# Conditioning by halves of the features, and the first four projections by chunks of features in four banks at once

## The reference

```
mod_l = silu(c) @ w_ada + b_ada          # 6 x 1024 values: shift, scale, gate, twice
mod_c = silu(c_ctx) @ w_ada + b_ada      # the same for 256 context tokens
hl = rms_norm(x, g_mix_norm) * (1 + sc1) + sh1
pl = hl @ w_in                           # queries, keys, values, Fourier part
hc = rms_norm(ctx, g_mix_norm) * (1 + csc1) + csh1
pc_kv = hc @ w_in[:, keys and values]
```

## Time and profile before

| | |
|---|---|
| time, median of 3 runs | 2213.22 us (2210.96 to 2216.42) |
| the profiled execution | 2213.58 us, of which the span of instructions is 2211.9 us |
| TensorE busy | 2134.6 us (97%) |
| VectorE busy | 1215.4 us (55%) |
| ScalarE busy | 702.6 us (32%) |
| data moved | 434.71 MB, mean 197 GB/s |
| first matmul of a projection | 37.77 us after the start |

### The profile page before, as it was taken

The page is one execution under the profiler, slowest core; times in us unless marked ns, Lnnn a source line. Parts: engine busy times, 40 slices in busy tenths (PEclk is TensorE's granted clock), DMA queues, the critical chain, the costliest instruction groups (busy, mean ns, idle before and its releaser), DMA issues.

```text
span 2211.9 us, 24806 instructions
## 1 busy us (share of the span) xinstructions
PE 2134.6 (97%) x9914; PEld 1428.7 (65%) x9914; DVE 1215.4 (55%) x1726; ACT 702.6 (32%) x1059; POOL 148.8 (7%) x157
## 2 busy tenths in 40 slices
PE   7999998997999989999999999999999999999997
PEld 3454444333333335678888888878777788888886
DVE  1776863344433336895474555566986646343434
ACT  4123422110000005323242231346884424232331
POOL 0011100002310004000000000000110000000000
PEclk9999999999999999999999999999999999999999
DMA  9756465999999993211345454423342222222221
GB/s 389 288 185 215 142 241 208 401 427 427 420 426 426 428 427 127 79 68 62 133 160 186 156 177 163 143 77 116 126 156 81 96 95 77 95 95 95 95 96 57
DMA packets 112808, 434.71 MB, mean 197 GB/s; under 512 B 7982, under 2 KB 13106, under 8 KB 98760
## 3 DMA queue, kind: packets, MB, share of 16 engines
q1 hardware_dynamic: 92872, 361.46, 42.6%
q0 software_dynamic: 19840, 71.93, 9.0%
HBM read 430.57 MB, written 6.36 MB: 198 GB/s over the span
## 4 chain that ended last, share of the span: by engine, by line
PE 60%; PEld 15%; DVE 7%; DMA 7%; issue 6%; ACT 2%; DVEq 2%; POOLq 0%; SPq 0%; PEldq 0%; POOL 0%; ACTq 0%
PE PS L1132 7%; PE PS L740 6%; PE PS L743 6%; PE PS L744 6%; PE PS L840 6%; PEld PS L740 5%; PEld PS L744 5%; PEld PS L743 4%; DMA work<-in_w_dn 4%; PE PS L1155 4%; PE PS L1399 3%; PE PS L1403 3%; PE PS L1402 3%; PE PS L1169 2%; PE PS L969 2%
## 5 line engine op out<-in xcount | busy, mean ns | idle before, releaser
L744 PE MATMUL PS<-work_f32r,work_f32r 128*128 128x512 f32 x1168 | 454.4, 389 | 0.0
L2155 DVE TENSOR_TENSOR ring_f32r<-ring,work_f32r 128x2048 fp32r<-128x2048 f32 x100 | 227.8, 2287 | 140.5 <-ACT work_f32r L1553 140.1
L740 PE MATMUL PS<-work_f32r,work_f32r 128*128 128x512 f32 x768 | 299.5, 390 | 2.1 <-DVE work_f32r L2902 1.1
L743 PE MATMUL PS<-work_f32r,ring_f32r 128*128 128x512 f32 x768 | 298.8, 389 | 0.0
L1553 ACT ACTIVATE work_f32r<-ring 128x2048 fp32r<-128x2048 f32 x100 | 190.2, 1910 | 304.0 <-DMA ring<-in_mlp_w 247.0
L744 PEld LDWEIGHTS PS<-work_f32r,work_f32r 128*128 128x128 f32 x1168 | 219.3, 188 | 45.6
L1132 PE MATMUL PS<-work 128*64 128x512 f32 x752 | 170.6, 597 | 2.2 <-ACT work L1761 2.2
L740 PEld LDWEIGHTS PS<-work_f32r,work_f32r 128*128 128x128 f32 x768 | 144.2, 188 | 33.3 <-DVE work_f32r L2902 1.5
L743 PEld LDWEIGHTS PS<-work_f32r,ring_f32r 128*128 128x128 f32 x768 | 144.2, 188 | 29.8 <-issue 0.2
L740 PE MATMUL PS<-h_f32r,work_f32r 128*128 128x512 f32 x400 | 155.9, 390 | 1.4 <-DVE work_f32r L2175 1.4
L743 PE MATMUL PS<-h_f32r,ring_f32r 128*128 128x512 f32 x400 | 155.6, 389 | 0.0
(11 more groups left out here) (423 smaller groups left out, 3357.8 us busy)
## 6 DMA issues: line engine op xcount, KB each, us to landing
work<-in_w_gu SPq DMA_DIRECT2D x47, 2048.0 KB, 21.9
ring<-in_mlp_w SPq DMA_DIRECT2D x64, 1024.0 KB, 5.2
work<-in_w_dn SPq DMA_DIRECT2D x24, 2048.0 KB, 24.6
ring<-in_w_gu SPq DMA_DIRECT2D x16, 2048.0 KB, 24.2
work<-in_ada_w_2T POOLq DMA_DIRECT2D x48, 512.0 KB, 3.6
work<-in_ada_w_2T POOLq DMA_DIRECT2D x16, 1536.0 KB, 6.8
ring<-in_m_w_in SPq DMA_DIRECT2D x20, 1024.0 KB, 5.2
work<-in_w_adaT POOLq DMA_DIRECT2D x8, 2048.0 KB, 10.4
```

The costliest lines, as they stand in the source:

```text
L740: mm = nc.tensor.matmul(PS[:, bank + k, :], f32r(w_of), f32r(hi(c)), start=first and c == 0, stop=False)
L743: nc.tensor.matmul(PS[:, bank + k, :], f32r(wlo), f32r(hi(c)), start=False, stop=False)
L744: mm = nc.tensor.matmul(PS[:, bank + k, :], f32r(w_of), f32r(lo(c)), start=False, stop=last and c == 3)
L2155: tt(f32r(ring[:, s, at, :]), ring[:, s, at, :], f32r(tiles[s][:, at, :]), ALU.subtract).then_inc(w_split, 1)
```

## The change

The conditioning is done in two halves of the features: transfers q = 0, 1 bring shift and scale for chunks 0 to 3 (q = 0 the upper four chunks of rows of `w_ada`, q = 1 the lower), q = 2, 3 for chunks 4 to 7. The columns of `w_ada` are reordered on the host to that end, and a row piece is 4 KB where it was 8 KB. The halves of the first `w_in` tile are issued after q = 1 and after q = 3. Each group of four matmuls covers two chunks of rows, so shift and scale come out as two partial sums that VectorE adds. The first norm takes the form of the later ones, but with a bank and a semaphore count of its own. The first four projections run over chunks in the outer loop and over the four banks in the inner one; the conditioning of the second half lies among them on TensorE, after chunks 1, 2 and 3. The context norm's sum follows all four. POOL's first loads of `w_adaT` wait for the last of the conditioning matmuls, as before.

```diff
-        w_early = [wk(2048, 2, 4 * TN), wk(6144, 2, 4 * TN), wk(20224, 2, 4 * TN), wk(24320, 2, 4 * TN)]
+        w_early = [wk(at, 4, 2 * TN) for at in (2048, 6144, 20224, 24320)]
...
-            load_tile(0, 0, 0, columns(A["w_in"]))
+            for q in range(4):
+                load_early(q)
+                if q % 2:
+                    half = q // 2
+                    sp.dma_start(ring[:, 0, 4 * half:4 * half + 4, :], rows(A["w_in"])[:, 4 * half:4 * half + 4, 0:TN]) \
+                        .then_inc(tile_loaded[half], 16)
...
-            pool.wait_ge(mod_mm, 1)
+            pool.wait_ge(mod_mm, COND + 2)
...
+            def first_norm():
+                for c in (0, KC - 1):
+                    if c:
+                        pe.wait_ge(sq_ready, KC)
+                    else:
+                        pe.wait_ge(sq_added, 1)
+                    for q in range(TC):
+                        nc.tensor.matmul(PS[32 * q:32 * q + 32, 6, 0:P], ones[:, 0:32], h[:, c, q * P:(q + 1) * P], start=(c == 0),
+                                         stop=(c > 0))
+                pe.drain().then_inc(ms_done, 1)
+                pe.wait_ge(in_small, 16 * 5)
+                pe.wait_ge(rstd_ready, 1)
+                for q in range(TC):
+                    mm = nc.tensor.matmul(PS[:, 7, q * P:(q + 1) * P], eye[:, 32 * q:32 * q + 1].broadcast_to([P, P]), inv_q,
+                                          start=True, stop=True)
+                mm.then_inc(mod_mm, 1)
+
+            def condition(q):
+                cols_half, rows_half = divmod(q, 2)
+                pe.wait_ge(in_mod[q], 16)
+                if q == 2:
+                    pe.wait_ge(mod_evac_and_spread, 1)
+                for c in range(4 * rows_half, 4 * rows_half + 4):
+                    for shift_or_scale in range(2):
+                        group = 2 * (c % 2) + shift_or_scale
+                        nc.tensor.matmul(PS[32 * group:32 * group + 32, 4, :], c_cols[:, c, :],
+                                         w_early[q][:, c % 4, shift_or_scale * TN:(shift_or_scale + 1) * TN],
+                                         start=(c < 2), stop=(c >= KC - 2))
+                if rows_half:
+                    pe.drain().then_inc(mod_mm, 1)
+
+            def conditions_turned(cols_half):
+                pe.wait_ge(mod_evac_and_spread, cols_half + 1)
+                if cols_half:
+                    pe.wait_ge(mods_ready, 1)
+                for b in range(4):
+                    mm = nc.tensor.transpose(PS[:, 5, b * P:(b + 1) * P], mod_rows[:, b * P:(b + 1) * P], eye)
+                mm.then_inc(mod_mm, 1)
+
             pe.wait_ge(consts_set, 1)
-            norm_sum(0, h, T)
-
+            keep_warm(3, 8)
             pe.wait_ge(cond_ready, 1)
...
+            first_norm()
+            condition(0)
+            keep_warm(3, 9)
+            condition(1)
+            keep_warm(3, 5)
+            conditions_turned(0)
+            keep_warm(3, 6)
...
-            features(0, 0, 0, h, T, 0)
-            features(1, 0, 1, h, T)
+            for c in range(KC):
+                if c % 4 == 0:
+                    pe.wait_ge(tile_loaded[c // 4], 16)
+                pe.wait_ge(h_ready, c + 1)
+                for e in range(4):
+                    mm = nc.tensor.matmul(PS[:, e, :], ring[:, 0, c, e * P:(e + 1) * P], h[:, c, :], start=(c == 0), stop=(c == KC - 1))
+                    if c == KC - 1:
+                        mm.then_inc(qkv_mm, 1)
+                if c == 1:
+                    condition(2)
+                elif c == 2:
+                    condition(3)
+                elif c == 3:
+                    conditions_turned(1)
             norm_sum(1, csq, CTX)
-            features(2, 0, 2, h, T)
-            features(3, 0, 3, h, T)
             tile_done()
...
-            norm_root(0, T)
-            act.wait_ge(mod_mm, 1)
-            copy(mod_rows, PS[:, 4, :]).then_inc(mod_evac_and_spread, 1)
-            act.wait_ge(mods_ready, 1)
-            norm_affine(0, h, gain[:, 0, :], mod1[:, 0:KC])
+            root_table(0)
+            act.wait_ge(ms_done, 1)
+            nc.scalar.activation(std_q, PS[:, 6, 0:P], ACT.Sqrt, scale=1.0 / D, bias=eps6).then_inc(std_ready, 1)
+            for cols_half in range(2):
+                act.wait_ge(mod_mm, COND + 2 * cols_half)
+                copy(mod_rows, PS[:, 4, :]).then_inc(mod_evac_and_spread, 1)
+                act.wait_ge(mods_ready, cols_half + 1)
+                for c in range(4 * cols_half, 4 * cols_half + 4):
+                    act.wait_ge(xn_ready, c + 1)
+                    nc.scalar.activation(h[:, c, :], h[:, c, :], ACT.Identity, scale=gain[:, 0, c:c + 1], bias=mod1[:, c:c + 1]) \
+                        .then_inc(h_ready, 1)
...
-            projected(0)
-            projected(1)
+            for e in range(4):
+                projected(e)
             norm_root(1, CTX)
...
-            norm_var(0, T, 1e-6)
-            norm_divide(0, x, h, T)
-            dve.wait_ge(mod_mm, 2)
+            dve.sem_inc(var_ready, 1)
+            for c in range(1, KC - 1):
+                add_square(0, h, c)
+            dve.wait_ge(std_ready, 1)
+            nc.vector.reciprocal(inv_q, std_q).then_inc(rstd_ready, 1)
+            dve.wait_ge(mod_mm, SPREAD)
...
+            def modulated(cols_half):
+                at = slice(4 * cols_half, 4 * cols_half + 4)
+                dve.wait_ge(mod_mm, TURNED + 2 * cols_half)
+                both = (mod1[:, 0:MOD_EARLY], 0), (modc[:], 1)
+                for dst, r in both:
+                    tt(of_half(dst, cols_half), turned_mods[:, 0:2, :, r], of_half(col("b_ada", 0, MOD_EARLY), cols_half), ALU.add)
+                dve.drain()
+                for dst, r in both:
+                    tt(of_half(dst, cols_half), turned_mods[:, 2:4, :, r], of_half(dst, cols_half), ALU.add)
+                dve.drain()
+                for n, (dst, r) in enumerate(both):
+                    done = stt(gain[:, n, at], dst[:, KC:2 * KC][:, at], 1.0, col("g_mix", 4 * cols_half, 4), ALU.add, ALU.mult)
+                done.then_inc(mods_ready, 1)
+
+            for cols_half in range(2):
+                for c in range(4 * cols_half, 4 * cols_half + 4):
+                    tt(h[:, c, :], x[:, c, :], PS[:, 7, :], ALU.mult).then_inc(xn_ready, 1)
+                modulated(cols_half)
             dve.wait_ge(h_ready, KC)
```

More of the change, by code:

```diff
@@ L160, in build @@
         lam_d, neglam = sm[:, 24:28], sm[:, 28:29]
-        eps5, std_q, inv_q = sm[:, 50:51], norm_buf[:, 0:P], norm_buf[:, P:2 * P]
+        eps5, eps6, std_q, inv_q = sm[:, 50:51], sm[:, 51:52], norm_buf[:, 0:P], norm_buf[:, P:2 * P]
         gsub = sm[:, 29:30]
@@ L332, in build @@
         AB, FR, FO = 2, 3, 4
+        SPREAD, COND, TURNED = 1, 2, 3
         score_mm, negmax_ready, exp_done, a_ready = sem("score_mm"), sem("negmax_ready"), sem("exp_done"), sem("a_ready")
@@ L419, in _, with load_early @@
             sp.dma_start(lam4, A["lam4"]).then_inc(in_small, 16)
-            for q in range(4):
-                sp.dma_start(w_early[q], rows(A["w_ada"])[:, 2 * q:2 * q + 2, :]).then_inc(in_mod[q], 16)
+            def load_early(q):
+                cols_half, rows_half = divmod(q, 2)
+                sp.dma_start(w_early[q], rows(A["w_ada"])[:, 4 * rows_half:4 * rows_half + 4, 2 * TN * cols_half:2 * TN * (cols_half + 1)]) \
+                    .then_inc(in_mod[q], 16)
             def load_tile(pair, i, s, source):
@@ L788, in joined_sum @@
                     else:
-                        pe.wait_ge(sq_added, k - 4)
+                        pe.wait_ge(sq_added, k - 3)
                     for q in range(TC):
@@ L795, in joined_sum @@
                     keep_warm(0, 9 if k > 5 else 6)
-                pe.wait_ge(rstd_ready, k - 3)
+                pe.wait_ge(rstd_ready, k - 2)
                 for q in range(TC):
@@ L856, in rope_half @@
                     nc.tensor.matmul(PS[:, 4 + j, :], rope_rot, src, start=True, stop=True).then_inc(rope_mm, 1)
-            tile_wait("in", 0, 0)
-            features(0, 0, 0, h, T, 0)
-            features(1, 0, 1, h, T)
+            for c in range(KC):
[12 more added lines that the diff above has]
+                    conditions_turned(1)
             norm_sum(1, csq, CTX)
-            features(2, 0, 2, h, T)
-            features(3, 0, 3, h, T)
             tile_done()
@@ L1630, in projected @@
                 copy(dst, PS[:, bank, 0:n]).then_inc(qkv_evac, 1)
-            projected(0)
-            projected(1)
+            for e in range(4):
+                projected(e)
             norm_root(1, CTX)
             norm_affine(1, cx, gain[:, 1, :], modc[:, 0:KC])
-            for e in range(2, 12):
+            for e in range(4, 12):
                 projected(e)
@@ L1742, in _ @@
             nc.scalar.activation(rstd_tok, rstd_tok, ACT.Sqrt).then_inc(std_ready, 1)
-            act.wait_ge(rstd_ready, 1)
+            act.wait_ge(rstd_ready, 2)
```

(15 more changed lines are left out.)

## The result

| | before | after |
|---|---|---|
| median of the runs | 2213.28 us | 2222.09 us (2220.56 to 2226.68) |
| ratio, 95% interval | | 1.0042 (1.0032 to 1.0052) |
| profiled execution, span | 2213.58, 2211.9 us | 2222.14, 2220.4 us |
| first projection begins | 37.8 us | 32.0 us |
| the context norm's sum ends | 55.2 us | 71.7 us |

The account below looks back on a forecast made before the run. It took TensorE, busy 97% of the span, as the bound, after `w_ada`'s last transfer until 31.0 us. −5.2 + 3.8 + 2.5 = +1.1, + 2.1 = +3.2 us: 2216.4 us on the median, range 2210.5 to 2222 us.

Parts of the forecast that it names:

- The start: Stretch before the first projection: it begins at 32.6 us instead of 37.77, 5.2 us sooner; bounds 29.9 and about 36.5 us.
- What moves in between: First projection to norm sum's end: 3.8 us of conditioning and 2.5 us turning added, end at 70.1 us, +1.1 us.
- the second turning: Before chunk 4, from transposes of the second conditioning half to the next projection: 2.5 us with TensorE doing nothing else.
- stay as many: Projections and norm sum: the 31.2 us of matmuls stay unchanged, since chunk order changes none of their sizes.
- The context norm comes late: VectorE's first `w_adaT` pass comes 14.9 us later, `rope(0)` ends at 106.9 us, TensorE waits at `rope_half(4)`: +2.1 us.
- TensorE [...] waits there 2.0 us, +2.1: At `rope_half(4)`: TensorE arrives at 104.9 us and waits for `rope(0)`, +2.1 us with hand-over; bounds 0 and 7.7 us.
- The slower rival: At `rope_half(4)`: late third and fourth `w_adaT` loads make the wait 7.7 us, +8.8, 2222.0 us; chance 0.12.
- The case of the banks in turn: First four projections: cycling banks costs clock, 27.7 us takes twice that, +31, 2244 us; chance 0.02.
- The case that the overlap pays: Clock rises early, projections start at 30 to 31 us, `rope_half(4)` hardly waits; 2211.6 to 2213.3 us; chance 0.24.
- best corner: Overlap rival's best outcome: projections start at 29.9 us, no wait at `rope_half(4)`, −1.6 us, 2211.6 us.
- all moves along: Behind `rope_half(4)`: attention and experts' loads shift with the delay, by 3 us, with no further wait counted.

Follow-up runs that it names:

- a_again: The changed kernel once more, unedited, on the same chip as a_compact_warm: 2223.16 us, ratio 1.0040 to the kernel before.
- a_warm_turn: The changed kernel with eight keep-warm matmuls behind the second turning, in TensorE's idle 1.9 us before chunk 4: 2221.73 us, ratio 1.0035.
- a_warm_both: As a_warm_turn, plus twenty keep-warm matmuls in front of the wait of `rope_half(4)`: 2220.86 us, ratio 1.0033.
- b_norm_new: The kernel before with only the first norm in the form of the later ones: 2214.34 us, ratio 1.0001.
- a_sum_early: The changed kernel with the context norm's sum behind chunk 5 instead of 7, and ScalarE's root before its four copies: 2216.27 us, ratio 1.0013.
- b_sum_late: The kernel before with the context norm's sum behind features 3, and ScalarE's four copies before its root: 2219.78 us, ratio 1.0026.
- a_compact: As a_sum_early, with second-half conditioning a chunk sooner, `condition(0)` before the first norm's spreading, three keep-warm matmuls for fourteen: 2208.50 us, ratio 0.9979.
- a_compact_warm: As a_compact, with sixteen keep-warm matmuls in front of the first norm's sum: 2208.33 us, ratio 0.9978.

## Why the prediction was wrong

**The start** was right: 32.0 us against 32.6, bound by TensorE's own list and not by the transfers. `condition(0)` met the rise of the clock and took 2.6 us, not 3.6 (3.64 us in a_again). That is read from durations, since the granted clock of the first 20 us differs between profiles that agree in them (last section).

**What moves in between** failed in one term. 1.9 to 2.0 us for each conditioning and 2.5 us for the second turning came as priced, and so did the idle 1.9 us. But the step took it that the matmuls "stay as many" and so cost the same, and gave no clock term to this idle stretch. The last four chunks took 15.67 us where 32 such records take 13.97 us: 1.7 us for the clock. The prediction's own rivals name both outcomes of an idle stretch of this length, the fall before 31.05 us and none at 24 to 26 us, but use them for the start alone. That the banks in turn aren't the cause is shown: in a_warm_turn, in a_warm_both and, with the idle stretch unfilled, in a_again they ran at 13.97 us, and in b_norm_new feature order took 15.67 us. That the idle stretch is the cause is likely and less firmly shown: in both kernels with the slow chunks the fall came behind one, but the same 1.89 us brought none in a_again and a_sum_early, so a profile with the stretch filled and no fall isn't a proof. With a start 0.6 us early, 1.7 us of clock and 0.5 us of small differences, the norm sum ended at 71.7 us and not 70.1.

**The context norm comes late** was the right mechanism, in the right place. b_sum_late shows that it alone makes the kernel before 6.2 us slower, and a_sum_early that undoing it gives 5.8 us back. The distance from the sum's end to VectorE's first pass was 5.5 us, as said. Here is the step that failed, "TensorE [...] waits there 2.0 us, +2.1", in two sizes. The fourth load landed after 10.6 us and not 8.6, so `rope(0)` ended 2.2 us later behind the sum than forecast, and the wait was 4.3 us. And the price of that wait was only its length: the rope matmuls behind it, 1.8 us longer at the lower clock, stood in no term. Why the fourth load took longer is open. Nothing else moved data beside the two loads; they moved it at some 400 GB/s up to 95.3 us, and the last part at 82 GB/s and less until 97.7 us. The time to landing also differs between executions (11.1 us in a_again, 9.4 in a_warm_both).

**The tally**: 3.2 us forecast, +1.6 at the end of the norm sum (−0.6 at the start, +1.7 clock, +0.5 small differences), +2.2 in the wait, +1.8 in the clock behind it, is 8.8 us; the first scores came 9.0 us later.

**The rivals.** The slower rival had the place and the sign, and its time (2222.0) met the measured one by luck. It gave 7.7 us to the wait, through a fourth load of 14.2 us. The wait was 4.3 us, and the clock, which the rival left out, cost 1.7 us before it and 1.8 us behind it. Its own condition, a landing later than 11.7 us (by the terms of the prediction it comes to 12.0), was not met. The case of the banks in turn is refuted here: they ran at 13.97 us per 32 records. For a bf16 kernel the Trainium skill (TensorE: Matmul & The Clock Gate, "A second HAM failure mode: psum-queue depth-cycling") says that going through the banks in turn left many small idle moments, and that the clock went back and forth. In these fp32 projections that didn't happen. The case that the overlap pays was open to a better order and not to this one: a_compact, at 2208.50 us, does better than its best corner of 2211.6. That corner's start, 29.9 us, comes to 30.2 by the terms given, and the six additions end at 16.5 us by theirs and not at 16.7; neither changes the forecast by more than 0.3 us.

**Beyond the first scores** the forecast that all moves along was right within 1 us: +9.0 there, +9.3 at the load behind attention, +8.5 in the span.

## What to carry to other kernels

An early start is worth only as much as the engine's list lets through: here the conditioning matmuls, free while they filled a wait, came to stand on the path, and one small sum moved behind the block held back another engine that the block's successor waits for. For every instruction that a reordering delays, ask who queues behind its result. With the sum two chunks sooner and the second conditioning one chunk sooner, the change is level with the kernel before (2212.37 us), and only with the shorter start as well is it faster (2208.50 us). Price a wait of TensorE at its length and, as a second case, with the matmuls behind it at the lower clock as well.

## What the runs showed of the hardware

Idle stretches of TensorE of 1.9 to 2.0 us had both outcomes. A fall of the clock came behind those of 1.89 us (after the change), 1.96 us (b_sum_late), 2.00 us (before) and 2.01 us (b_norm_new), and none behind 1.89 us (a_again, a_sum_early) and 1.95 us (before). So it differs between executions of one kernel, and between two stretches of one execution. At `rope_half(4)` the lower clock came with all four unfilled waits of 3.8 to 4.8 us (after, a_again, a_warm_turn, b_sum_late). It made the eight rope records 1.8 us longer, or 2.8 to 2.9 us where nearly all of them ran at the lower level. Keep-warm matmuls in that wait kept it away in the one kernel that had them (a_warm_both).

Of two 2 MB loads of `w_adaT` issued 4.6 us apart with nothing else moving data, the first landed after 8.2 us and the second after 10.6 us (after the change). In a_again it was 8.1 and 11.1 us, in a_warm_both 8.4 and 9.4 us.

The granted clock of the first 20 us can't be relied on in these profiles. At 16 to 18 us it is 1.00 after the change and 0.50 in a_again, with the same 1.08 us for the sum of the first norm, where the full clock gives 0.64 us (a_compact_warm). There the level is read from durations.
